# One core, two transformer blocks: another order at the head of the token stage, two weight loads moved, constant products in five waits of TensorE

## The reference, cut to what matters

```python
mod = c_act @ ada_w[i] + ada_b[i]                       # modulation stage
h = rmsnorm(x, norm_mix_g[i]) * (1 + sc1) + sh1
x = x + g1 * conformer_conv(h, ...)                     # conv stage, front stage
h = rmsnorm(x, norm_ffn_g[i]) * (1 + sc2) + sh2
x = x + g2 * hier_moe(h, ...)                           # router stage, expert stage
x = rmsnorm(x, final_g)                                 # token stage from here
h = rms_norm(x, norm_g[l]) * (1.0 + scale) + shift
proj = h @ w_in[l]                                      # token stage: q, k, indexer, dt
q = partial_rope(rms_norm(q, q_norm_g[l]), cos_a, sin_a)
```

## Time and profile before

| what | us |
|---|---|
| median of the runs | 2631.97 |
| profiled execution | 2634.09 |
| its span | 2632.4 |
| PE busy | 2408.7 (92%) |
| DVE, ACT, POOL busy | 1591.8, 1128.6, 790.8 |
| mean granted clock of PE | 0.961 |
| PE waits for a DMA ahead of the last taps (284.18) | 3.36 |
| PE waits for ACT in the front stage (f_acc) | 3.0 |

### The profile page before, as it was taken

How to read it: one execution, slowest core, us unless ns; L and a number is a source line. 1 busy time by engine, 2 the same in 40 slices (tenths; PEclk the granted TensorE clock), 3 DMA queues, 4 the chain that set the end, 5 groups by cost and what they waited for, 6 DMA issues and landing times. The chain is left out here.

```text
span 2632.4 us, 49136 instructions
## 1 busy us (share of the span) xinstructions
PE 2408.7 (92%) x19345; PEld 1252.9 (48%) x19345; DVE 1591.8 (60%) x2637; ACT 1128.6 (43%) x1815; POOL 790.8 (30%) x915
## 2 busy tenths in 40 slices
PE   4999896899899996779999989799999999999999
PEld 3555544455455553345444434344444444444544
DVE  6787776222222223476499999735756747747853
ACT  6110454232223333555556558514634724715720
POOL 2012021333333333332355522101611702603502
PEclk8999897999999998889899999899999999999999
DMA  8686658699999998310112239632002011020133
GB/s 251 183 271 227 226 169 341 241 408 408 409 409 381 406 407 313 97 64 17 39 42 80 96 98 198 189 123 107 9 2 104 9 50 55 9 89 25 65 120 128
DMA packets 213450, 451.71 MB, mean 172 GB/s; under 512 B 112656, under 2 KB 122256, under 8 KB 204816
## 3 DMA queue, kind: packets, MB, share of 16 engines
q1 hardware_dynamic: 171360, 368.02, 39.3%
q0 software_dynamic: 23344, 43.67, 5.2%
q10 hardware_dynamic: 18560, 37.39, 4.1%
HBM read 371.07 MB, written 58.94 MB: 163 GB/s over the span
## 5 line engine op out<-in xcount | busy, mean ns | idle before, releaser
L2860 POOL TENSOR_TENSOR group_words<-group_words 128x1024 f16<-128x1024 f16 x64 | 153.0, 2413 | 377.4 <-PE i_pj L146 368.2
L1587 PE MATMUL m_gu<-arena,m_xT 128*32 128x256 f32 x2880 | 234.1, 390 | 6.4 <-DMA arena<-in_moe_w_up 6.4
L1667 DVE TENSOR_TENSOR m_xT<-m_xm,row_gain 128x256 f32<-128x256 f32 x89 | 38.0, 427 | 306.3 <-PE m_gu L1587 306.3
L144 PE MATMUL i_pj<-hT,group_words 128*128 128x512 f16 x384 | 146.3, 381 | 13.4 <-ACT group_words L354 7.7
L1587 PEld LDWEIGHTS m_gu<-arena,m_xT 128*32 128x32 f32 x2880 | 118.3, 112 | 66.9 <-issue 18.0
L1642 ACT ACTIVATE m_sg<-m_gu 64x256 f32<-64x256 f32 x88 | 33.6, 382 | 265.1 <-PE m_gu L1587 265.1
L144 PE MATMUL s_pj<-hT,arena 128*128 128x512 f16 x368 | 141.1, 383 | 5.8 <-issue 5.8
L146 PE MATMUL i_pj<-hT,group_words 128*128 128x512 f16 x384 | 146.3, 381 | 0.0
L145 PE MATMUL i_pj<-hT,group_words 128*128 128x512 f16 x384 | 146.3, 381 | 0.0
L145 PE MATMUL s_pj<-hT,arena 128*128 128x512 f16 x368 | 141.1, 383 | 0.0
L146 PE MATMUL s_pj<-hT,arena 128*128 128x512 f16 x368 | 140.9, 383 | 0.0
(11 more groups left out here) (642 smaller groups left out, 6632.9 us busy)
## 6 DMA issues: line engine op xcount, KB each, us to landing
arena<-in_moe_w_down SPq DMA_DIRECT2D x17, 2048.0 KB, 24.9
arena<-in_moe_w_up SPq DMA_DIRECT2D x16, 2048.0 KB, 22.3
arena<-in_moe_w_gate SPq DMA_DIRECT2D x16, 2048.0 KB, 24.5
x_tok<-in_ada_w ACTq DMA_DIRECT2D x8, 2048.0 KB, 12.3
conv_y<-in_moe_w_gate SPq DMA_DIRECT2D x7, 2048.0 KB, 28.4
conv_y<-in_moe_w_up SPq DMA_DIRECT2D x7, 2048.0 KB, 15.5
hT<-in_moe_w_gate SPq DMA_DIRECT2D x6, 2048.0 KB, 26.1
hT<-in_moe_w_up SPq DMA_DIRECT2D x6, 2048.0 KB, 22.1
```

The source lines that it names most:

```text
L144: nc.tensor.matmul(out, lhsT=lh, rhs=rh, start=start, stop=False)
L1587: last = nc.tensor.matmul(gu_ps[tile(j), 0:FFN // 2], lhsT=xT[:, c % 2, c // 2, :], rhs=expert_unit(k, e, part)[:, c, halves[i]], start=c ...
L1667: nc.vector.tensor_tensor(xT[:, :, :, :], xm[:, :, :, :], of_rows(shift), ALU.add).then_inc(xt_sb, 1)
L2860: return tuple(k.nc.gpsimd.tensor_tensor(k.y_U[:, t % 2, n], k.adt_parts[:, n, t, heads].unsqueeze(2).to_broadcast([P, HPG, P]), k.upto16. ...
```

## The change

`keep_busy(k, bank, n)` issues n f16 products of the constants table with itself, 128 x 128 by the bank's columns, into a PSUM bank that is not read; they wait for nothing. It is called at five places (62 products): 15 ahead of `sums(2)` and 8 ahead of `sums(3)`, in front of a conv stage with 7 ahead of its first products; 9 of 440 columns ahead of `taps(last)`; 14 ahead of the front stage's wait for `gate_sb`; 9 ahead of tile 4.

Units 6 and 7 are issued by SP in the expert stage, behind `dest_nat` and `gates_nat` and a wait for the third gather, ahead of `ends_ready`. The last round's `y` stores are issued by ACT behind its loop over blocks; POOL keeps only the releases.

```diff
-            load_unit(k, sp, 6)          # router_stage, SP
-            load_unit(k, sp, 7)
...
+            sp.wait_ge(x_in[2], 16)      # experts_stage, SP
+            load_unit(k, sp, 6)
+            load_unit(k, sp, 7)
             sp.wait_ge(k.ends_ready, 1)
...
+                act.wait_ge(y_read, last * RING + i + 2)
+                act.dma_start(k.slot_out[...], y[:, i, :]).then_inc(k.last_stored, 16)
```

```diff
+            nc.scalar.activation(k.gate_half[:, HALF - 1:HALF], k.const("ones")[:, 0:1], ACT.Sqrt)
             act.wait_ge(k.y_done, 4 * blocks_of(act))
-            for c in range(6):
+            for c in range(5):
                 split(c)
             squares(0)
             weighed_squares(0)
             roots(0)
+            split(5)
+            residual(0)
+            first_high()
             split(6)
             split(7)
-            high_tokens(0)
-            residual(0)
...
-            for t in range(4):
+            for t in range(AHEAD):       # POOL; AHEAD = 3
                 if t:
                     weigh(t)
                 fetch1(t + 1)
-                if t in (1, 3):
-                    low_tokens(t if t == 1 else 2)
+                if t == 2:
+                    low_tokens(1)
                 fetch0(t + 2)
+            heads(0)
+            weigh(AHEAD)
+            low_tokens(2)
+            fetch1(AHEAD + 1)
...
             add_rows(0)                  # DVE
             first_weigh()
-            split(4)
             variances(0)
             normalise(0)
+            split(4)
+            first_low()
             split(5)
+            add_rows(1)
             split(6)
-            first_low()
-            add_rows(1)
             split(7)
```

More of the change, by code:

```diff
@@ L170, in late_sums_of, with keep_busy @@
     return k.late_sums[:, n, :]
+def keep_busy(k, bank, n):
+    table = k.consts[:, :, :].rearrange("p a q -> p (a q)").bitcast(F16)
+    for _ in range(n):
+        k.nc.tensor.matmul(bank, lhsT=table[:, 0:P], rhs=table[:, 0:bank.shape[-1]], start=True, stop=True)
 def half_shift(k):
@@ L1564, in _ @@
             pool.sem_inc(x_copied, 1)
[L1565 to L1568, removed]
+            for i in range(2, RING):
+                give(i, last * 16)
         @block.tensor
@@ L1645, in _ @@
                     .then_inc(ht_sb, 1)
+            last = ((blocks + FULL) & FULL) >> 2
+            for i in range(RING):
+                act.wait_ge(y_read, last * RING + i + 2)
+                act.dma_start(k.slot_out[bass.ds((last * RING + i) * BLOCK, BLOCK), :].rearrange("r (j c) -> j r c", j=4),
+                              y[:, i, :]).then_inc(k.last_stored, 16)
         @block.vector
@@ L1806, in tokens_stage @@
             row0[:, 0].bitcast(F16).rearrange("p (b c q) -> p b c q", b=2, c=KC)
+        half_full, half_high, half_low = (k.sem(f"q_half_{n}") for n in ("full", "high", "low"))
+        unread = tp[:, 2:4].rearrange("p a n -> p (a n)")
         h_turned, h_full, h_high, h_low = (k.sem(f"q_h_{n}") for n in ("turned", "full", "high", "low"))
@@ L1889, in _ @@
                 for n in range(4):
+                    if t == n == 1:
+                        turn(2)
                     if n == 3 and t + 2 < TT:
@@ L1915, in squares @@
                 act.wait_ge(summed, t + 1)
-                nc.scalar.activation(row1[:, :], k.x_tok[:, t, :], ACT.Square,
+                nc.scalar.activation(unread if t < AHEAD else row1[:, :], k.x_tok[:, t, :], ACT.Square,
                                      accum_out=sums[:, t % 2, 0:1]).then_inc(x_squared, 1)
@@ L1942, in high_tokens, with first_high @@
                 act.wait_ge(h_full, t + 1)
-                if t == 0:
+                nc.scalar.copy(k.hT[:, 0, :, t * P:(t + 1) * P], full).then_inc(h_high, 1)
+            def first_high():
+                act.wait_ge(h_turned, 1)
+                for h in range(2):
+                    half = slice(4 * h, 4 * h + 4)
+                    for c in range(4 * h, 4 * h + 4):
+                        last = nc.scalar.activation(full[:, c, :], tp[:, c // 4, (c % 4) * P:(c % 4 + 1) * P], ACT.Identity,
+                                                    scale=gain[:, c:c + 1], bias=shift[:, c:c + 1])
+                    last.then_inc(half_full, 1)
+                    act.wait_ge(half_full, h + 1)
                     act.wait_ge(low, 2)
-                nc.scalar.copy(k.hT[:, 0, :, t * P:(t + 1) * P], full).then_inc(h_high, 1)
+                    nc.scalar.copy(k.hT[:, 0, half, 0:P], full[:, half]).then_inc(half_high, 1)
+                act.sem_inc(h_full, 1)
+                act.wait_ge(half_high, 2)
+                act.sem_inc(h_high, 1)
             def evacuate(t, n):
@@ L2128, in first_low @@
             def first_low():
-                dve.wait_ge(h_high, 1)
                 dve.wait_ge(low, 4)
-                v.tensor_tensor(k.hT[:, 1, :, 0:P], full, k.hT[:, 0, :, 0:P], ALU.subtract).then_inc(h_low, 1)
+                for h in range(2):
+                    half = slice(4 * h, 4 * h + 4)
+                    dve.wait_ge(half_high, h + 1)
+                    v.tensor_tensor(k.hT[:, 1, half, 0:P], full[:, half], k.hT[:, 0, half, 0:P],
+                                    ALU.subtract).then_inc(half_low, 1)
+                dve.wait_ge(half_low, 2)
+                dve.sem_inc(h_low, 1)
             def variances(t):
```

88 lines of the change are left out of this document (46 added, 42 removed).

## The result

The changed kernel takes 2611.26 us, the median of four runs (2608.71 to 2612.12), against 2632.19 for the kernel before (four runs, one more than the three behind 2631.97): a ratio of 0.9918, interval 0.9907 to 0.9930, or 18.4 to 24.5 us less. The profiled execution has a span of 2609.4, 23.0 less. The forecast was 2601, in the range 2593 to 2615: the direction is right, the token stage brought most of the gain as forecast, and two thirds of the whole came.

A forecast was written before the change was run, and what follows sets the result against it. Up to 1131 the chain of single operations preparing tokens sets the end, after it PE and its loop. -3.8 - 23.7 - 3.7 = -31.2 gives 2602.9 on the profile, 2600.8 on the median's footing; range 2593 to 2615.

The forecast's parts named there:

- Expert stage, -3.8: Start of experts: moving loads 6 and 7 empties the DMA queue, so the copy releasing PE starts 3.8 us earlier.
- Rival C: Expert weight stream: moved 4.19 MB miss the quiet window, experts run 10.2 us late, 2614.8; chance 0.07.
- Token head, -3.3 up to turn(0): Start of token stage: earlier store landing and reordered splits bring turn(0) to 1054.6 from 1057.85, 3.3 us earlier.
- The landing: Last stores on ACT's queue, before the first token fetch: they land 4.0 us after the last issue, at 1039.3.
- Halves, -2.8 more: Token tile 0: only half the preparation precedes the first product, so turn(0) to product takes about 4.9 us, before 7.71.
- Tile 1, -12.8: Token tile 1: earlier fetches and a later turn(2) start its products at 1083.2 instead of 1096.0, 12.8 us earlier.
- Tile 2, -24.9: Token tile 2: heads(0) after three prepared tiles starts transposes(0) at 1105.4, 24.9 us earlier; 23.7 at the stage's end.
- rival D: Token loop: POOL's products hold more DVE operations, the period grows and the kernel is slower, 2644.5; chance 0.06.
- Fillers, -3.7: Constant products in PE's waits keep its clock up: conv -1.2, taps -2.5, front stage and tile 4 0; sum -3.7.
- the 2.5 at the taps: Last taps: nine fillers in PE's 3.4 us wait let 48 products take 2.5 us instead of 5.00.
- E: Rival: fillers don't hold the clock and the last stores land no earlier, 2606.4; chance 0.17.
- B: Rival in the token stage: POOL's four operations in a row bind tile 2, only tile 1's 12.8 stays, 2611.7; chance 0.12.

The follow-up runs named there:

- the last set: Changed kernel with last stores by SP, final_g behind them, chunk 5's low part earlier (2604.23 us), and versions less one part; without constant products 2604.04.
- the run with all three edits: Changed kernel with last stores by SP, final_g loaded behind their landing, chunk 5's low part ahead of tile 0's halves: 2604.23 us, ratio 0.9897.

## Why the prediction was right or wrong

**Expert stage, -3.8.** Right at the copy (3.9 of the 6.0 us there lie between the first gather and the copy), and alone 3.7. But this size too rests on one profile: in the five that have units 6 and 7 in the router stage the copy waits 3.88, 3.86, 3.44, 2.39 and 1.75 us, and the kernel before had the longest. The bound of 0 was needed for another reason than I gave: the stream of weights, full from 505 on, takes back 1 to 3 us. Rival C, experts late by 10, did not come.

**Token head, -3.3 up to turn(0): this step failed**, with 0.3 measured. It mis-sized three terms. *ACT.* The sum has the splits 2.7 us after the experts, which leaves room for one issue behind the last y and the table. They start 4.4 after: the four issues in a row end 2.05 after the last expert product, and behind the table ACT does the Sqrt and then stands idle for 0.86. DVE's low splits, which end 14.9 after the experts for the 13.1 of the sum, were last, as forecast. *final_g*, moved behind the first fetched row, was costed at nothing: DVE waits 1.44 us for it. These two, 1.7 and 1.4, are the 3.0 that are missing. *The landing*, 4.0 us as on quiet engines, was wrong too, since the first fetch is 5.8 after ACT's last issue and gains 0.9, not 3; but in the changed kernel it cost nothing, as DVE's splits were later. The runs show the first two: final_g earlier brings turn(0) 1.5 sooner, stores on SP with that 4.6 to 5 sooner. The stores alone made it 1.2 later, but by the rows and not by the splits.

The Trainium skill's sentence on queues (Trainium Kernel Development and Optimization, "Key Constraints": issuing from several queues saves only the issue time) is what the prediction's other value, a landing near 1042.5, came from. The first fetch came at 1036.17, which is 1042.3 counted from the experts of the kernel before (6.1 later), so the trace agrees in the number. That all queues land alike is not shown: from the end of the last issue to the first fetch it took 6.5 us by POOL and 8.6 by ACT with final_g and the small tables beside the stores, and 4.6 by POOL, 5.8 by ACT and 3.7 and 3.9 by SP with those behind them. So the loads beside them did cost the stores 2 to 3 us, as the forecast had it, and ACT's queue lost 1.2 of that again; why it is the slowest stays open.

**Halves, -2.8 more.** Right: 5.06 for 4.9.

**Tile 1, -12.8 from the last expert product on.** 6.9 measured (13.0 less 6.1). 3 of the missing 6 is the head's, and the rest is, in the main, the 3.14 us that PE waits for POOL's low part. It stands in a chain that I took from POOL alone: tile 1's rows are added by DVE behind tile 0's halves and a split, and DVE's variances wait behind two splits that POOL's weighing holds, 6.46 us for 4.3. Tile 1's residual comes behind that, POOL's next fetch waits for its store until 1076.10, and the low part comes only behind this fetch and another weighing, 4.1 us after ACT has the high part. No run put the low part ahead of them, so what that order alone costs stays open. The Trainium skill (SBUF — State Buffer, "Who interferes with whom": a DVE operation with two SBUF inputs and a GpSimd operation that reads SBUF lock each other out) gave 2.4 us for this collision; the trace agrees, with 2.1 us more for DVE and 0.9 for POOL, in every profile with this order. I left it out of the sum, since no row of before showed a split held; it belonged in. No run moved the weighing away from the splits, so its price at the end is read from traces only.

**Tile 2, -24.9, and -23.7 at the stage's end.** 16.7 (transposes(0) start at 1107.46, 22.8 earlier, less 6.1) and 17.4. Almost all that is missing at the end (6.3) was missing at tile 1's first product already (5.9): from there to the end the stage wins 10.5 us, and I had 10.9. So the order did what was forecast. heads(0) is squared ahead of tile 3, and tile 0's reduction comes 13.7 us nearer to tile 1's first product. transposes(0) then stand behind PE's own tile 1, with 2.14 us of waiting for turn(3), and win 9.8 there for the 12.1 of the sum. Of the loop I had the period (23.7) and that one more tile runs at it (half of 2.2 is 1.1, not 1.2). What I had not priced is the first period's 26.3. In the trace its tensor_scalar is held 2.81 us, rival D's mechanism at one place in place of five; the loop's other holds, 1.83 and some 2.97 a period, are in both kernels. No run took that hold away, and the 10.5 for 10.9 leaves little for it at the end: there the errors of the terms nearly cancel.

**Fillers, -3.7.** 1.6 alone, 0 in the last set, neither clear of nothing. (The bounds of the four parts add up to -6.3 and +4.7, not -5.7 and +5.) Locally most do as told: the windows of the changed kernel's modulation and conv stages (columns as in rows 3) are

```profile
44.00:52.00 8.00, 5.75 (x41) 4.47 (x42) 5.96 (x10) 2.55 (x5) 0.15 (x1) 0.96 0.01 2
52.00:54.10 2.10, 2.10 (x6) 0.71 (x5) 1.48 (x3) 2.10 (x4) 0.38 (x1) 0.50 0.49 101
282.00:287.00 5.00, 5.00 (x95) 5.00 (x92) 4.85 (x7) 0.61 (x2) 0.28 (x1) 1.00 0.28 68
```

The clock holds almost to 52 and at the taps, and falls between: the seven at 52 run at 0.50 and end 0.7 us late. The first conv products behind them then run at full clock and make that good: the ninth starts at 56.57, before at 57.44. The fourteen of the front stage take 3.18 us at full clock, where I had 6 at half, and PE's wait there falls from 3.0 to 0.3. But of the 5.2 us at the front stage's products 3.1 are lost before the gathers. A piece of ada_w gains 3.7 only, and 48 one-column sums behind it take 8.1 us for 6.1: the clock, 0.85 from 420 to 425, is 0.50 from 425 to 430. This is not the constant products' doing: the sums take 8.1 in the run with all three edits less these products, 6.6 in the same with them, and 5.8 with them alone. DVE's wait and PE's sums, after:

```profile
411.30 0.49 DVE L202 TENSOR_SCALAR f_sums<-arena,csilu 128x512 f32<-128x512 f32 x1 [4.86 <-DMA arena<-in_ada_w]
```

```profile
420.96 4.68 PE L215 MATMUL late_mods<-consts,f_sums 128*128 128x1 f32 x32
425.51 1.85 PE L215 MATMUL late_mods<-consts,gate_half 128*128 128x1 f32 x8
427.21 1.84 PE L215 MATMUL late_mods<-consts,steps 128*128 128x1 f32 x8
```

The step that failed is the one from "no wait of PE for a DMA is large from here to the experts" to "what these stages gain reaches the end": it was DVE that waited, for a piece of ada_w. And the 2.5 at the taps, most of the sum, was priced on the longest wait of the five.

**Range and chances.** 2611.3 is outside the forecast's own range, 2595 to 2606, which had 0.58, and inside the whole one, above E (2606.4) and just below B (2611.7). B's size came by luck: it is the sum of a head that gained nothing, a longer chain to tile 1 and fillers that gave little, and not POOL's four operations. E's two conditions came in part, but E has neither ACT's delay, final_g nor the collision.

## What to carry to other kernels

When an issue is moved to another engine, count when the last issue can end there, and look at what is behind it: the same four stores stood 3.6 us in ACT's queue at the one moment when ACT was wanted, and on SP and POOL the splits started at once. A gain that rests on how long one transfer took in one profile is worth its mean over several, not its largest. And where a chain crosses two engines, follow it through each engine's own order: tile 1 hung on two splits that it does not read.

## What the runs showed of the hardware

The first stages end at a different time from one execution to the next. In four profiles on one chip, with the same code up to there, the first gather of the experts came at 455.45, 457.08, 457.80 and 458.58 us. Over all it came at 456.7 to 459.7 in the five profiles without constant products and at 455.5 to 458.6 in the nine with them, means 458.7 and 456.7; gains of that size are lost in it.

Four DVE operations with two inputs each beside one POOL product took nearly the sum of both times, 6.45 or 6.46 us for 4.3 and 2.4, in all ten profiles of the changed order.

A store issued by ACT holds its queue for 0.55 to 0.56 us, and the first of the four for 1.19; one by POOL takes 0.69, one by SP 0.54. ACT's splits did not begin right behind the stores: 2.4 us later in the changed kernel, behind the table and the Sqrt, and 1.9 later with the stores alone (38.81 behind 36.87), where the profile shows nothing between.
